# Key copies by transfers inside SBUF, and value products without their zero halves, in a two-block transformer kernel

## The reference, cut to what matters

```python
# second block: 16 heads of 64 features, chunks of 64 positions, own chunk and 8 before it
q = rms_norm(q.reshape(b, nc, CHUNK, N_HEADS, HEAD_DIM), q_norm_g)
k = rms_norm(k.reshape(b, nc, CHUNK, N_HEADS, HEAD_DIM), k_norm_g)
scores = jnp.einsum('bnqhd,bnkhd->bnhqk', q, kb) * scale + bias
scores = jnp.where(valid, scores, NEG_INF)
probs = jax.nn.softmax(scores, axis=-1)
out = jnp.einsum('bnhqk,bnkhd->bnqhd', probs, vb)
```

## Time and profile before

| | before |
|---|---|
| median of 3 runs | 2145.02 us (2144.67 to 2146.3) |
| profiled execution | 2145.05 us |
| its span, first to last instruction | 2143.3 us |
| PE busy | 2125.5 us, 99% |
| DVE, ACT, POOL busy | 1507.6, 956.1, 1007.2 us |
| granted clock of TensorE, mean | 0.999 of full speed |
| attention of the second block | about 765 to 1235 us of the span |

### The profile page before, as it was taken

One profiled execution on the slowest core, in us unless ns is written; L12 is line 12 of the kernel. 1 busy time (PEld: TensorE's weight loads), 2 busy tenths in 40 slices (PEclk: granted clock), 3 DMA queues, 4 the chain that ended last, 5 costly groups with the idle time before them and its releaser, 6 DMA issues.

```text
span 2143.3 us, 28233 instructions
## 1 busy us (share of the span) xinstructions
PE 2125.5 (99%) x10402; PEld 1782.4 (83%) x10402; DVE 1507.6 (70%) x2619; ACT 956.1 (45%) x1714; POOL 1007.2 (47%) x697
## 2 busy tenths in 40 slices
PE   9999999999999999999999999999999999999999
PEld 8888888888888888888888888788878888888887
DVE  6776774354875457878778668433877887898886
ACT  5554524433332256666666522212555455433331
POOL 3232465555555533122131156547566564666564
PEclk9999999999999999999999999999999999999999
DMA  7320114332234253333333166314144435836432
GB/s 233 106 77 21 46 59 177 123 133 79 79 118 156 95 140 89 87 85 110 86 90 105 50 221 235 98 58 183 47 165 157 167 137 187 314 109 236 145 117 111
DMA packets 198439, 269.66 MB, mean 126 GB/s; under 512 B 57944, under 2 KB 116088, under 8 KB 198176
## 3 DMA queue, kind: packets, MB, share of 16 engines
q1 hardware_dynamic: 126992, 205.58, 27.8%
q10 hardware_dynamic: 71312, 62.30, 9.5%
HBM read 191.23 MB, written 85.00 MB: 129 GB/s over the span
## 4 chain that ended last, share of the span: by engine, by line
PE 93%; DVE 3%; POOL 1%; ACT 1%; issue 1%; DMA 1%; DVEq 0%; ACTq 0%; SPq 0%; POOLq 0%
PE ps L205 80%; PE ps L2404 3%; PE ps L2379 3%; PE ps L2391 2%; PE ps L777 1%; PE ps L752 1%; PE ps L763 1%; POOL w_lo L3281 1%; PE ps L2416 1%; DVE a_lo L447 1%; PE ps L687 0%; DMA qk_raw<-qkv_tm 0%; DVE prob L2701 0%; PE ps L2916 0%; PE ps L1478 0%
## 5 line engine op out<-in xcount | busy, mean ns | idle before, releaser
L205 PE MATMUL ps<-a_hi,w_hi 128*128 128x512 f32 x1312 | 507.8, 405 | 2.7 <-DVE a_lo L447 1.2
L160 POOL TENSOR_TENSOR w_hi<-w_raw,zero 128x512 fp32r<-128x512 f32 x156 | 187.7, 1233 | 675.6 <-PE ps L205 562.1
L205 PE MATMUL ps<-a_hi,w_lo 128*128 128x512 f32 x1312 | 490.7, 392 | 0.0
L205 PE MATMUL ps<-a_lo,w_hi 128*128 128x512 f32 x1312 | 488.5, 390 | 0.0
L205 PE MATMUL ps<-w_hi,a_hi 128*128 128x512 f32 (+1 forms) x960 | 369.0, 384 | 3.8 <-POOL w_lo L673 2.0
L205 PE MATMUL ps<-w_hi,a_lo 128*128 128x512 f32 (+1 forms) x960 | 367.4, 383 | 0.0
L205 PE MATMUL ps<-w_lo,a_hi 128*128 128x512 f32 (+1 forms) x960 | 367.0, 382 | 0.0
L205 PEld LDWEIGHTS ps<-a_hi,w_lo 128*128 128x128 f32 x1312 | 246.1, 188 | 54.3
L205 PEld LDWEIGHTS ps<-a_hi,w_hi 128*128 128x128 f32 x1312 | 246.6, 188 | 43.5 <-DVE a_lo L447 2.7
L205 PEld LDWEIGHTS ps<-a_lo,w_hi 128*128 128x128 f32 x1312 | 247.2, 188 | 38.0
L165 POOL TENSOR_TENSOR w_lo<-w_raw,w_hi 128x512 fp32r<-128x512 f32 x156 | 224.1, 1467 | 3.1
(11 more groups left out here) (308 smaller groups left out, 4083.2 us busy)
## 6 DMA issues: line engine op xcount, KB each, us to landing
mlp_part<-u_parts SPq DMA_DIRECT2D x26, 1024.0 KB, 7.3
w_raw<-in_w_in_dram SPq DMA_DIRECT2D x21, 1024.0 KB, 5.3
u_parts<-mlp_acc SPq DMA_DIRECT2D x28, 512.0 KB, 2.8
u_parts<-res SPq DMA_DIRECT2D x28, 512.0 KB, 2.8
feat_fm<-stage ACTq DMA_DIRECT2D x52, 256.0 KB, 2.0
conv_in<-feat_fm ACTq DMA_DIRECT2D x24, 512.0 KB, 5.2
qkv_raw<-in_w_in_dram SPq DMA_DIRECT2D x11, 1024.0 KB, 5.4
res<-in_x_dram SPq DMA_DIRECT2D x16, 512.0 KB, 6.4
```

Of the source, the lines that this page charges most:

```text
L160: hi = nc.gpsimd.tensor_tensor(w_hi[slot][:, k:k + 2, :], w_raw[:, k:k + 2, :], zero[:, 0:1].unsqueeze(2).to_broadcast([P, 2, CW]), ALU.add)
L205: last = nc.tensor.matmul(out_of(o), lhs, rhs(o), start=first and n == 0, stop=final and n == 2)
```

## The change

- `k_high` makes only the lower copy (partitions 64 to 127) by an activation. ScalarE then waits until that activation has ended (`hi_r`), and issues a transfer from SBUF to SBUF that copies the 64 x 512 numbers to partitions 0 to 63. Head 0 is still done with two activations.
- `k_low` on VectorE makes only the lower copy, at nn = 4, and at step 0 of the head itself. `copy_k_low` issues the transfer for the other one from ScalarE's queue, at the end of ScalarE's step nn = 5, and at the end of step 1 of the head itself.
- TensorE waits for both copies through `k_copied` ahead of the first `scores` that reads them.
- `v_low` moves from nn = 6 to nn = 5.
- `values` multiplies first the key blocks that both windows share, over 256 columns, then the others over the 128 columns that belong to them. The eight memsets at the start of the phase go.

```diff
@@ values (TensorE)
-                        first, last_kb = window(2 * g)[0], window(2 * g + 1)[1] - 1
-                        for kb in range(first, last_kb + 1):
+                        even, odd = range(*window(2 * g)), range(*window(2 * g + 1))
+                        both = [(kb, 0, 256) for kb in even if kb in odd]
+                        one = [(kb, 0, P) for kb in even if kb not in odd] + [(kb, P, 256) for kb in odd if kb not in even]
+                        for kb, c0, c1 in both + one:
...
-                                last = nc.tensor.matmul(ps[:, O_BANK, 0:256], v_st[:, h, kb, :], pt[:, sl, :],
+                                last = nc.tensor.matmul(ps[:, O_BANK, c0:c1], v_st[:, h, kb, :], pt[:, sl, c0:c1],
@@ body (TensorE)
-                                    pe.wait_ge(lo_r, i * 4 + (2 * ((n + 2) // 8) + (n + 2) % 8 // 4 + 2))
+                                    head, r = i * 2 + (n + 2) // 8, (n + 2) % 8 // 4
+                                    pe.wait_ge(lo_r, head * 2 + (r + 2))
+                                    if head:
+                                        pe.wait_ge(k_copied, 32 * ((head - 1) * 2 + (r + 1)))
@@ k_high, copy_k_low (ScalarE)
-                        for side in (1, 0):
-                            nc.scalar.activation(k_hi[side * HD:(side + 1) * HD, slot, cols],
-                                                 ps[HD:P, T_BANK, :], ACT.Copy, scale=gains[HD:P, 0:1]).then_inc(hi_r, 1)
+                        if head == 0:
+                            nc.scalar.activation(k_hi[0:HD, slot, cols], ps[HD:P, T_BANK, :], ACT.Copy,
+                                                 scale=gains[HD:P, 0:1])
+                        nc.scalar.activation(k_hi[HD:P, slot, cols], ps[HD:P, T_BANK, :], ACT.Copy,
+                                             scale=gains[HD:P, 0:1]).then_inc(hi_r, 1)
+                        if head:
+                            act.wait_ge(hi_r, 2 * (head * 2 + r) + 2)
+                            act.dma_start(k_hi[0:HD, slot, cols].bitcast(F32), k_hi[HD:P, slot, cols].bitcast(F32)).then_inc(k_copied, 16)
+
+                    def copy_k_low(head, slot, r):
+
+                        act.wait_ge(lo_r, head * 2 + (r + 2))
+                        cols = slice(r * 512, (r + 1) * 512)
+                        act.dma_start(k_lo[0:HD, slot, cols].bitcast(F32), k_lo[HD:P, slot, cols].bitcast(F32)).then_inc(k_copied, 16)
@@ body (ScalarE)
+                                if nn == 5:
+                                    copy_k_low(head, slot, 0)
...
+                            if n < STEPS and nn == 1 and not (first and n < 8):
+                                copy_k_low(i * 2 + hh, hh % 2, 1)
@@ body (VectorE)
-                                if nn in (4, 5):
-                                    k_low(head, slot, 0, nn - 4)
-                                if nn == 6:
+                                if nn == 4:
+                                    k_low(head, slot, 0, 1)
+                                if nn == 5:
                                     v_low(head, slot)
-                            if n < STEPS and nn < 2 and not (first and n < 8):
-                                k_low(i * 2 + hh, hh % 2, 1, nn)
+                            if n < STEPS and nn == 0 and not (first and n < 8):
+                                k_low(i * 2 + hh, hh % 2, 1, 1)
```

More of the change, by code:

```diff
@@ L2319, in phase_attention @@
                 hi_v, lo_v = S("hi_v"), S("lo_v")
+                k_copied = S("k_copied")
                 dve_self = S("dve_sel")
@@ L2399, in values @@
                         pe.wait_ge(o_done, i * 8 + (m // 2 + 1))
-                        first, last_kb = window(2 * g)[0], window(2 * g + 1)[1] - 1
-                        for kb in range(first, last_kb + 1):
+                        even, odd = range(*window(2 * g)), range(*window(2 * g + 1))
+                        both = [(kb, 0, 256) for kb in even if kb in odd]
+                        one = [(kb, 0, P) for kb in even if kb not in odd] + [(kb, P, 256) for kb in odd if kb not in even]
+                        for kb, c0, c1 in both + one:
                             sl = kb - (2 * g - back) + nslot * (m // 2 % 2)
                             for pt in (pt_hi, pt_lo):
-                                last = nc.tensor.matmul(ps[:, O_BANK, 0:256], v_st[:, h, kb, :], pt[:, sl, :],
-                                                        start=(kb == first and pt is pt_hi),
-                                                        stop=(kb == last_kb and pt is pt_lo))
+                                last = nc.tensor.matmul(ps[:, O_BANK, c0:c1], v_st[:, h, kb, :], pt[:, sl, c0:c1],
+                                                        start=((kb, c0, c1) == both[0] and pt is pt_hi),
+                                                        stop=((kb, c0, c1) == one[-1] and pt is pt_lo))
                         last.then_inc(valued, 1)
@@ L2612, in _ @@
                         dve.sem_inc(s_, n_)
[L2614 to L2617, removed]
                     nc.vector.memset(bias[0:HD, :, wmax - HD:wmax], NEG)
@@ L2624, in q_low @@
                     def q_low(head, slot, r):
-                        dve.wait_ge(hi_r, 3 * (head * 2 + r) + 1)
+                        dve.wait_ge(hi_r, 2 * (head * 2 + r) + 1)
                         cols = slice(r * 512, (r + 1) * 512)
@@ L2630, in k_low @@
                     def k_low(head, slot, r, side):
-                        dve.wait_ge(hi_r, 3 * (head * 2 + r) + 3)
+                        dve.wait_ge(hi_r, 2 * (head * 2 + r) + 2)
                         cols = slice(r * 512, (r + 1) * 512)
```

## The result

| | us |
|---|---|
| kernel before, median of 4 runs | 2145.49 (2144.67 to 2146.3) |
| changed kernel, median of 4 runs | 2160.62 (2158.28 to 2162.01) |
| ratio | 1.0070 (1.0057 to 1.0083) |
| profiled execution after: span, time | 2158.5, 2160.34 |

Slower by 15 us, where 2.4 were forecast, and outside the range. The spans of the two profiled executions differ by 15.2 us (2158.5 - 2143.3), and these have to be found. TensorE makes 10402 products in both, in the same order but for the key blocks within a value group, so the start of the n-th can be compared: the changed kernel is 0.4 us ahead at 780 us, 15.3 behind at 1240 and 15.2 at the end. So 15.7 us arise in the attention of the second block, and nothing behind it.

What follows compares the result with a forecast made beforehand. TensorE's own products, busy in 99% of the span, were taken as the bound. From 2145.05 us, -1.5 (zero halves) + 4.5 (ScalarE's queue) + 0.7 (copies' arrival) - 1.3 (VectorE) = +2.4 gave 2147.4 us; range 2141 to 2154.

Steps and rivals of the forecast that it cites:

- the queue hold at nn = 7: ScalarE's queue, 14 places: the wait for `k_hi`, copy and three loads delay the next step's `high()`; +4.5 us.
- The slack of 0.39 us: Lateness of `pt_hi` that does not reach TensorE's next `turn`: of 0.60 us late, 0.21 reached it.
- Part 2: ScalarE's queue order, with the wait and copies ahead of loads and `high()`: +4.5 us.
- The long issues: Three of the 14 places where the loads take 3.3 to 4.7 us to issue, not 1.96: 1.6 us added.
- the queue holds `high()` with its present issue times: Rival for ScalarE's queue: slow load issues stay slow when shifted, hold 8.6 us; +8.1, 2153.2 us; chance 0.24.
- The hold is hidden: Rival: quicker `pt_lo` with VectorE unburdened, and the queue's delay made good; -3.7, 2141.4 us; chance 0.08.
- Part 1: Zero halves in TensorE's value products: 192 go from 256 to 128 columns, saving 0.01 us each at most; -1.5 us.
- Both rivals that priced a product over 128 columns at 0.06 or 0.085 us: Value products: cut ones save -10.2 or -6.7 us, giving 2138.8 or 2142.3 us in all; chance 0.05 each.
- Part 3: The copies' arrival before the scores: late once, behind bias transfers in the same queue; +0.7 us (0 to +3).
- Part 4: VectorE loses 30 `k_low` of 756 ns, so TensorE waits less for `pt_lo`; -1.3 us (-2.9 to +0.5).

Runs made afterwards that it cites:

- e1: The changed kernel with the second half's `k_hi` copy issued one step later, at the end of step 0 of the head itself: 2144.83 us.
- e7: The kernel before with only the second half's `k_hi` copy at step 7 made by transfer, with the wait ahead of it: 2157.2 us.
- e3: The kernel before with only the new `values` (zero halves left out) and without the eight memsets: 2143.57 us.
- e6: The changed kernel with the 256-column value products and the memsets of before: 2162.78 us.
- e2: The changed kernel with the three loads of step 7 issued ahead of the wait for `k_hi` and the copy: 2145.95 us.
- e9: The changed kernel with only the first half's `k_lo` copy by transfer; `k_hi` and the second half of `k_lo` made twice on the engines: 2143.99 us.
- e5: The changed kernel with `k_hi` made by two activations as before, without that wait; `k_lo` copies still by transfer: 2143.75 us.
- e4: The kernel before plus only ScalarE's queue waiting for the first `k_hi` activation of the second half, no copy by transfer: 2151.32 us.
- e8: The kernel of e1 with each of the 60 copies issued a second time into a spare tile that nobody reads: 2151.7 us.

## Why the prediction was wrong

The sum gave 2147.4 us, the range ended at 2154, and 2160.6 were measured. The bounds of the terms added up to 2157.2, and the range was cut below that; even the bounds were too low.

**The place and the mechanism were right.** The forecast named the queue hold at nn = 7, its places and the row that would show it; e1 and e7 confirm that it is most of the loss. The slack of 0.39 us held too, in the changed kernel: 1.40 late cost 1.00, 0.88 cost 0.48, 0.30 cost nothing.

**The step that failed is the size of Part 2:** +4.5 forecast, 11.6 measured as the hold (0.2 of it there before). It splits so:

- *The chain at the twelve places with a free way: +2.4.* From `k_hi`'s end to `pt_hi` I added up 2.49 us; measured are 2.60 to 2.96, 2.75 in the mean. The copy's issue was taken from a store to DRAM, 0.36 us and 0.04 to the next; it is 0.48 and 0.10. In four places the loads took 2.1 to 2.3 us for 1.96. Where the slack is used up, every tenth of a us counts in full.
- *The adding up of the places: +1.2.* The distances from `k_hi` to the transposes' end were read rightly (three of 1.2 us, two of 1.7, nine of 1.9 to 2.4), but the costs were added up wrongly. Three times 0.84 and twice 0.25 are more than 2.9 already; by the prediction's own rule (2.49 us less the distance, less 0.03, less 0.39) the places of the kernel before cost 3.9 us, and the twelve with the distances as they came 4.1.
- *The long issues: +3.4.* I allowed 1.6 us, because the loads would come 2.2 us later and meet less of the weight load. One of the three got shorter (3.32 us before, 1.99 after, at the sixth place). The other two got longer: 4.96 us for 4.73 at the third place and 4.28 for 3.92 at the last, 5.04 us of hold in these two. The weak step was to scale a stall from the single reason seen beside it.

**Left out of the sum:** that the granted clock can fall to half round a long wait of TensorE (two waits of over 2 us, about 3 us), and that the loads, held back by the wait, can come late themselves (`v_raw`, 1.2 us). Part 2 spoke of `high()` behind the loads, and never asked who waits for the loads.

**The rival "the queue holds `high()` with its present issue times"** was this outcome's mechanism, with 0.24; its 8.6 us of hold and 2153.2 us were too small for the same reasons. *The hold is hidden* falls with `turn`'s waits at ten of the 14 places.

**Part 1:** -1.5 forecast, -1.9 in e3 (0 to -3.9), and -1.6 by the attention of its trace: near the forecast, but less than the times can tell from nothing. Both rivals that priced a product over 128 columns at 0.06 or 0.085 us would have made e3 2135.3 or 2138.8 us (10.2 or 6.7 below before); they fall.

**Part 3:** +0.7 forecast, +2.3 measured, in the bounds, but at other places: not behind the bias transfers in the same queue but beside the weight load in SP's. The Trainium skill ("DMA: Bandwidth & Descriptors", "Issuing engines are not separate DMA queues") says that transfers of all issuing engines share the 16 DMA engines and interleave; this case's trace agrees, with 6.7 us for 128 KB beside 1 MB and 2.2 us with the way free.

**Part 4:** -1.3 forecast. Outside the 14 places `turn` waited 2.8 us for `pt_lo` before (1.27, 0.37 and 1.15) and 1.15 in the changed kernel (0.40, 0.29 and 0.46): -1.6, near the forecast.

**What e6 has over e7.** It is 6.1 us of span. Compared product by product, 5.2 of them arise in the attention: 3.0 of hold, 2.4 of late copies, 1.1 of half clock behind a wait of 3.65 us, less 1.6 of waiting for `pt_lo`. Another 1.2 us lie behind the attention, near 1362 us, where products (L205) wait for VectorE's `a_lo` (L447), 2.0 us in five places for 1.2 in three. The same happens in e1, e2 and e9, where the products fall back by 1.4 us or so, and not in e3, e5, e7 or the changed kernel. It does not go with the number of copies (e9 has 15, the changed kernel 60), its cause is open, and without it e1's span would not be above e3's.

**What stays open.** That the stalls and the traffic make each other worse is suggested by the third place (hold 3.8 us in e6, 1.7 in e7), but one execution of each doesn't show it, and which transfer lengthens which issue was not separated.

## What to carry over

Before a DMA queue is made to wait for its own engine, list every entry behind the wait up to the next activation that another engine needs: their issue times add up, and the sum decides (e2 puts three loads ahead and pays nothing measurable, e7 leaves them behind and pays 11.9 us). On a kernel whose TensorE is 99% busy, price such a wait with the longest issue seen at the place, not with a hoped-for shorter one, and look at the granted clock round the longest waits: here two stretches of some 3 us at half clock cost up to 1.5 us each. A copy inside SBUF in place of an activation is not free work: 0.58 us of the issuing queue against 0.68 us of its engine, and 2.2 us of delay that becomes 6.7 beside a large load.

## What the runs showed of the hardware

- ScalarE's queue issues transfers ahead of activations that stand before them, as long as nothing waits: in e1 the last load is issued 0.44 us before `k_hi` starts. The wait takes this lead away: in e4, with nothing but the wait, that is 5.6 us.
- The granted clock fell to 0.50 (1.2 GHz) for some 3 us round long waits of TensorE: in the wait of 2.70 us itself (0.74 in 860 to 861, then 0.50), within a us of the end of the waits of 1.98 us in e4 and 3.65 us in e6, and some 1.5 us after the end of the waits of 2.02 us (1186.57, in the changed kernel) and 1.94 us (e8). Behind waits of 1.23 us (the changed kernel), 1.52 (e7), 1.70 (e4), 1.71 and 1.84 (e8, 939.60 and 1100.57) it stayed 1.00.
- A copy of 128 KB inside SBUF: 0.48 us to issue, 2.2 us to land; 6.1 and 6.7 us when issued 0.3 and 0.1 us behind 1 MB of weights in the other queue.
- In a row of products over 128 columns with new weights each, all but the first follow by 0.10 to 0.12 us, as those over 256 do (0.12); at half clock both follow by 0.21 to 0.22 us.
